# Attention steps that run on across head groups, and query units with three 256-wide products in half a PSUM bank a tile

## What is computed

```python
# layer 0: sliding-window attention with sinks; layer 1: NSA attention; after each a conv FFN
proj = h @ w_in                      # h: 256 x 2048; 32 query heads of 64, in 4 groups of 8
s = q @ k.T - slope * dist           # per head, 256 queries x up to 256 keys
p = softmax(s)                       # layer 0: with a sink in the denominator
o = p @ v                            # layer 1: gate0*o_cmp + gate1*o_sel + gate2*o_win
mix = o @ w_o
x = x + rmsnorm(mix, g[1])
h = rmsnorm(x, g[2])
x = x + rmsnorm((silu(conv(h @ w_gate)) * (h @ w_up)) @ w_down, g[3])
```

## Time and profile before

| what | value |
|---|---|
| median of 3 runs | 2227.19 us (2223.99 to 2230.46) |
| the profiled execution's own time | 2230.99 us |
| its span, first to last instruction | 2229.3 us |
| PE matmul busy | 2167.5 us (97%) |
| DVE, ACT, POOL busy | 1353.7, 1084.3, 249.9 us |
| mean granted TensorE clock | 0.987 |
| DMA | 381.14 MB, mean 171 GB/s |

### The profile page before, as it was taken

How to read it: one execution, slowest core, us unless ns; L and a number is a source line. 1 busy time by engine, 2 the same in 40 slices (tenths; PEclk the granted TensorE clock), 3 DMA queues, 4 the chain that set the end, 5 groups by cost and what they waited for, 6 DMA issues and landing times.

```text
span 2229.3 us, 34314 instructions
## 1 busy us (share of the span) xinstructions
PE 2167.5 (97%) x11619; PEld 1807.2 (81%) x11619; DVE 1353.7 (61%) x2087; ACT 1084.3 (49%) x1639; POOL 249.9 (11%) x395
## 2 busy tenths in 40 slices
PE   8999999999999999999989998999999999999998
PEld 7777888888888888888777776888888888888887
DVE  7655577676767654447754444467666766664444
ACT  6765454444444444445455555454444444443443
POOL 3351000000000000003005544000000000000000
PEclk9999999999999999999999999999999999999999
DMA  6434545656565565554562222545555555565553
GB/s 210 138 122 170 189 152 179 198 179 197 173 201 181 192 207 189 189 189 167 174 208 76 69 73 86 179 160 184 186 189 186 188 188 182 194 207 189 189 188 124
DMA packets 107195, 381.14 MB, mean 171 GB/s; under 512 B 14114, under 2 KB 14578, under 8 KB 106482
## 3 DMA queue, kind: packets, MB, share of 16 engines
q1 hardware_dynamic: 104962, 373.69, 50.5%
q10 hardware_dynamic: 2160, 6.46, 0.8%
HBM read 377.97 MB, written 2.14 MB: 171 GB/s over the span
## 4 chain that ended last, share of the span: by engine, by line
PE 91%; DVE 5%; issue 2%; ACT 1%; POOL 1%; DMA 0%; DVEq 0%; ACTq 0%; POOLq 0%; SPq 0%
PE set L541 36%; PE set L609 29%; PE set L545 18%; PE set L727 2%; PE set L709 1%; PE set L750 1%; DVE wlo L1302 1%; DVE scored L1579 1%; PE set L638 1%; POOL probs L496 1%; PE set L711 1%; PE set L743 0%; PE set L702 0%; PE set L753 0%; ACT whi L935 0%
## 5 line engine op out<-in xcount | busy, mean ns | idle before, releaser
L541 PE MATMUL set<-hs,whi 128*128 128x512 f32 x3584 | 1215.5, 402 | 18.6 <-DVE wlo L1302 7.1
L1302 DVE TENSOR_TENSOR wlo<-raw,whi 128x1024 fp32r<-128x1024 f32 x704 | 857.9, 1229 | 564.8 <-ACT whi L935 563.6
L935 ACT ACTIVATE whi<-raw 128x1024 fp32r<-128x1024 f32 x704 | 738.9, 1057 | 764.5 <-PE set L545 408.8
L545 PE MATMUL set<-hs,wlo 128*128 128x256 f32 x3584 | 853.9, 281 | 0.0
L545 PEld LDWEIGHTS set<-hs,wlo 128*128 128x128 f32 x3584 | 672.9, 190 | 78.1
L541 PEld LDWEIGHTS set<-hs,whi 128*128 128x128 f32 x3584 | 620.7, 190 | 115.3 <-issue 15.6
L609 PE MATMUL set<-whi,hid 128*128 128x512 f32 x1408 | 387.0, 395 | 0.0
L609 PEld LDWEIGHTS set<-whi,hid 128*128 128x128 f32 x1408 | 264.6, 188 | 63.5 <-DVE wlo L1302 0.6
L609 PE MATMUL set<-wlo,hid 128*128 128x512 f32 x704 | 222.4, 395 | 0.0
L609 PEld LDWEIGHTS set<-wlo,hid 128*128 128x128 f32 x704 | 132.4, 188 | 31.6
L609 PE MATMUL set<-whi,os 128*128 128x512 f32 x512 | 145.7, 398 | 0.0
(11 more groups left out here) (180 smaller groups left out, 1194.9 us busy)
## 6 DMA issues: line engine op xcount, KB each, us to landing
raw<-in_stream SPq DMA_DIRECT2D x704, 512.0 KB, 3.3
gain_rows<-rows ACTq DMA_DIRECT2D x4, 1024.0 KB, 5.2
xT<-in_x SPq DMA_DIRECT2D x8, 256.0 KB, 8.2
out_y<-out_f SPq DMA_DIRECT2D x3, 512.0 KB, 2.7
bo_rows<-rows ACTq DMA_DIRECT2D x1, 1024.0 KB, 8.0
wg_raw<-in_w_gates ACTq DMA_DIRECT2D x1, 768.0 KB, 4.3
out_y<-out_f SPq DMA_DIRECT2D x2, 256.0 KB, 2.4
w2k_sb<-in_w ACTq DMA_DIRECT2D x2, 128.0 KB, 7.6
```

Of the source, the lines that this page charges most:

```text
L541: return mm(sets[set_of(u)][:, t, 0:2 * w], whi[:, slot, cols], r, start=first, stop=final)
L545: return mm(sets[set_of(u)][:, t, w:2 * w], wlo[:, slot, cols], r[:, 0:w], start=False, stop=False)
L935: A(whi[:, slot, :], raw[:, slot, :], ACT.Copy).then_inc(hi_ready, 1)
L1302: V.tensor_tensor(wlo[:, slot, :], raw[:, slot, :], whi[:, slot, :].bitcast(F32), ALU.subtract).then_inc(lo_ready, 1)
```

## The change

1. The loops over g are written out, so operands are addressed directly (`k_dup`, `v_nat`, `kc_all`, `gates`, `sinks_sb`), and `stage` and its tiles are gone. POOL keeps only the product that makes `vc_g` (`mask_values`).
2. `attention_steps` numbers the pairs of a layer through: step m of the next group follows on the last one of the group before, at an even distance of 32 slots per group (layer 0: 4 slots a half step; layer 1: 1.78), starting at slot 3. The fill is in the first group and the drain after the last one only. In the output unit the last group's half steps stand in slots 3 to 23.
3. `q_unit` replaces `unit` for the queries: three matmuls of 256 columns per tile and k-tile (`whi` x high, `whi` x low, `wlo` x high), all summed in the same half bank. Four tiles take two banks, and successive query units alternate between banks 0, 1 and banks 2, 3; each waits only for the unit before the last.
4. ACT has no part in reading the queries out. DVE makes `qg` from PSUM in one pass: layer 0 four `tensor_scalar` of 256 columns, layer 1 two `scalar_tensor_tensor` of 512 columns. The first two tiles end half a k-tile earlier (`q_first`).

```diff
-def attention_slots(layer, last):
-    halves = 2 * (len(attention_pairs(layer)) + LAG + 1)
-    lo, hi = (0, 23) if last else (1, 30)
-    at = [[] for _ in range(CH * UT)]
-    for k in range(halves):
-        at[lo + k * (hi - lo) // (halves - 1)].append((k // 2, k % 2))
-    return at
+def attention_steps(layer):
+    per, slots = len(attention_pairs(layer)), CH * UT
+    last = (GROUPS - 1) * per
+    final = 2 * (per + LAG + 1) - 1
+    at = [[[] for _ in range(slots)] for _ in range(GROUPS)]
+    for k in range(2 * (GROUPS * per + LAG + 1)):
+        m, h = divmod(k, 2)
+        if m < last:
+            slot = FIRST_SLOT + k * slots // (2 * per)
+        else:
+            slot = (GROUPS - 1) * slots + FIRST_SLOT + (k - 2 * last) * (LAST_SLOT - FIRST_SLOT) // final
+        at[slot // slots][slot % slots].append((m, h))
+    return at
...
+            def q_unit(u, waits=None, tile_before=None, after_chunk=None):
+                g = (u - Q0) if u < O0 else (u - Q1)
+                banks = [2 * (g % 2), 2 * (g % 2) + 1]
+                for c in range(CH):
...
+                    for j in range(CK):
+                        kt = CK * c + j
+                        r = hs[:, kt, :]
+                        if kt == KT - 1:
+                            turns = [(t, i) for t in range(UT) for i in range(3)]
+                        else:
+                            turns = [(t + a, i) for t in (0, 1) for i in range(3) for a in (0, 2)]
+                        for n, (t, i) in enumerate(turns):
+                            if tile_before and n % 6 == 0:
+                                tile_before(c * UT + j * CK + n // 6)
+                            if kt == 0 and n == 0:
+                                if g >= 2:
+                                    pe.wait_ge(evacuated, UT * (u - 1))
...
+                            w = (wlo if i == 2 else whi)[:, slot, cols]
+                            ins = mm(sets[0][:, banks[t // 2], (t % 2) * S:(t % 2 + 1) * S], w, r[:, S:2 * S] if i == 1 else r[:, 0:S],
+                                     start=kt == 0 and i == 0 and t % 2 == 0, stop=kt == KT - 1 and i == 2 and t % 2 == 1)
...
-                with pe.Fori(0, GROUPS - 1) as g:
-                    unit(q0 + 1, hs, lp=(g, CH, UT), tile_before=attention(layer, g * UT + UT * (q0 + 1), g, False))
+                for g in range(GROUPS - 1):
+                    q_unit(q0 + 1 + g, tile_before=attention(layer, g))
...
-                    add(0)
-                    for t in range(UT):
-                        if t + 1 < UT:
-                            add(t + 1)
-                        dve.wait_ge(q_summed, more_e + (UT * (u - q0) + t + 1))
-                        V.scalar_tensor_tensor(qg[:, t, :], half[:, st, t, :], -HD ** -0.5, rnorm[:],
-                                               ALU.mult, ALU.mult).then_inc(evacuated, 1)
+                        bank = sets[0][:, 2 * (g % 2) + half_unit, :]
+                        if layer == 1:
+                            V.scalar_tensor_tensor(qg[:, 2 * half_unit:2 * half_unit + 2, :],
+                                                   bank.rearrange("p (t s) -> p t s", t=2), -HD ** -0.5, row_of_r(2),
+                                                   ALU.mult, ALU.mult).then_inc(evacuated, 2)
+                            continue
```

More of the change, by code:

```diff
@@ L84, in halves_before @@
 def halves_before(u):
-    return UT * (u - sum(u >= b for base in (O0, DN0, O1, DN1) for b in range(base + 1, base + 5)))
+    without = [b for base in (O0, DN0, O1, DN1) for b in range(base, base + 4)]
+    without += [b for base in (Q0, Q1) for b in range(base, base + GROUPS)]
+    return UT * sum(v not in without for v in range(u))
 def attention_items(layer):
@@ L509, in next_bias @@
                         nc.gpsimd.tensor_scalar(t, t, 0.25, 1.0, ALU.mult, ALU.mult).then_inc(bias_ready, 1)
[L511 to L517 removed]
+                for m in range(PAIRS[layer]):
+                    normalize(m)
+                    next_bias(m)
+                    if pair_item(layer, m)[1] == "cmp" and m > 0:
+                        mask_values(group_pair(layer, m)[0])
                 ff = FF0 if layer == 0 else FF1
@@ new lines, in attention, with scores @@
+            def attention(layer, host):
+                items = attention_items(layer)
+                q0 = (Q0, Q1)[layer]
+                at = attention_steps(layer)[host]
+                def scores(m):
+                    i, kind = pair_item(layer, m)
+                    g = group_pair(layer, m)[0]
+                    if m >= 1:
+                        pe.wait_ge(scores_read, item(layer, m, 0))
+                    if m == 0:
+                        pe.wait_ge(k_dup_ready, 1 if layer == 0 else 3)
@@ L1137, in step @@
+                def step(tile):
+                    for m, h in at[tile]:
+                        o = m - LAG - 1
+                        if h == 1 and o >= 0 and pair_item(layer, o)[1] in ("swa", "win"):
                             pair_high(o)
-                        if LAG <= n < len(pairs) + LAG and h < len(pairs[n - LAG]):
-                            copy_turned(n - LAG, h)
-                        if n < len(pairs) and h < len(pairs[n]):
-                            exponents(n, h)
@@ L1143, in attention, with attention_unit @@
-                return step
-            def attention_unit(u, evac, step, lp=None):
-                more, turn, _ = loop_terms(lp)
+                        if LAG <= m < PAIRS[layer] + LAG and h < len(pair_heads(layer, m - LAG)):
+                            copy_turned(m - LAG, h)
+                        if m < PAIRS[layer] and h < len(pair_heads(layer, m)):
+                            exponents(m, h)
+                return step
+            def attention_unit(u, evac, step):
                 g0 = first_chunk(u)
@@ L1246, in _ @@
                     act.dma_start(rows.rearrange("n (k f) -> (n k) f", f=P), post_rows[0:5 * KT, :]).then_inc(rows_made, 16)
-                with act.Fori(0, GROUPS - 1) as g:
-                    lp = (g, CH, UT)
-                    attention_unit(q0 + 1, q_evac(q0 + 1, lp), attention(layer, g, False), lp)
+                for g in range(GROUPS - 1):
+                    attention_unit(q0 + 1 + g, lambda: None, attention(layer, g))
                 n = 2 * layer
```

407 lines of the change are left out of this document (187 added, 220 removed).

## The result

| | before | after |
|---|---|---|
| median | 2228.82 us (2223.99 to 2231.96, 4 runs) | 2190.69 us (2188.55 to 2193.26, 4 runs) |
| span of the profiled execution | 2229.3 us | 2191.5 us |
| ratio | | 0.9837, 95% interval 0.9815 to 0.986 |

The kernel is 38.1 us faster by the medians (36 by the ratio, whose interval is about 31 to 41). The two profiled executions differ by 37.8 us of span. The prediction said 2196, in a range of 2181 to 2214.

A forecast was written before the change was run, and what follows sets the result against it. PE, busy 97% of the span, was taken as the bound. Savings of 11.5, 8.7 and 12.2 us less losses of 1.0 and 0.5 gave -30.9 us, 2200 profiled, 2196 after taking off 3.8; range 2181 to 2214.

The forecast's parts named there:

- The likeliest case: Whole kernel: the terms as summed, 2196 us, own range 2188 to 2204, chance 0.58.
- a: Query-unit starts: alternating banks remove PE's waits for DVE to clear PSUM, 12.2 us less 0.7 left; 11.5 us saved.
- b: Query hosts: steps that run on cut PE's 11.7 us of waits for probabilities to 3.0; 8.7 us saved.
- c: Layer 1, 1172 to 1345: clock falls (mean 0.92) after the removed waits go, except one; 12.2 us saved.
- d: Layer 1's output unit: missing fill saves, closer steps and doubled turns cost; 1.0 us lost, bounds 6 saved, 8 lost.
- e: Query units: three 256-column products with three loads replace 512 plus 256 with two; 0.5 us lost in all.
- Every sign named for them: No unit-start wait for `qg`, at most tenths in slot 3; layer 1 query-host POOL waits under 3 us, longest group 0.
- The rival that the chain binds again: Attention flow: DVE, ACT and POOL need the 3.6 us left, b saves nothing, half of c returns; 2210 us, chance 0.20.
- The fall that was left for group 0: Layer 1's pipeline fill: one clock fall stays after a 1.5 us wait, priced at 1.6 us.
- the 5 to 9 foretold: Layer 1's output unit: 5 to 9 us of PE waits would remain, most of them for POOL.
- 3 x 0.117 = 0.351: Query units: three 256-column products at 0.117 us each take 0.351 us, against 0.350 for the former pair.
- slow rival: Query units: weight loads not hidden between 256-column products; at 0.190 us each, 112 us more, 2308 us; chance 0.08.

The follow-up runs named there:

- wide product run: Changed kernel with a tile's two 256-column high-weight products in the query units made one of 512 (query values differ): 2187.07 us, ratio 0.9824.

## Why the prediction was right, and where its terms were off

The likeliest case came, with 5 us more than it said. Term by term, measured between the two profiled executions, which are 37.8 us apart:

| term | predicted | measured | from |
|---|---|---|---|
| a, b: PE's idle time | -20.2 | -19.8 | windows: 7.5 in layer 0, 11.1 in layer 1's hosts; 1.2 at the joint ahead of them |
| c: clock | -12.2 | -12.4 | 161.4 less 149.0 |
| d: output unit | +1.0 | 0.0 | idle +0.6 in layer 1, -0.5 in layer 0 |
| e: 256-wide products | +0.5 | +3.6 to +4.7 | wide product run |
| left out | 0 | about -10 | the remainder |

**a and b.** Every sign named for them came: no wait for `qg` at a unit's start or in slot 3, waits for POOL in the query hosts of layer 1 of 2.8 us, the longest (1.30) in group 0. The sum of a and b was right, their split was not. (Of the 4.1 us that b read for layer 0's query hosts, 1.4 stand in its output unit.) The prediction subtracted each wait from its own row, as if one could be had without the other. With the banks alone idle time in layer 1's hosts falls by 1.5 us (slots 3 to 30) or 3.8 us (slots 1 to 30) and the turns' waits grow; with the steps alone it falls by 8.6; with both by 11.1. The rival that the chain binds again, 2210 us, is close to what happens with the banks alone (2213 and 2211). It didn't come in the changed kernel; b's account, that steps that run on just give the chain the time that it needs (3.6 us against 3.6), fits the waits that are left, which are small but not gone.

**c.** The size was right for the profiled execution, and the fills show that it is the clock and not something that goes with the waits: the same products behind the same joints, with PE kept busy, took 8.0 us less. The fall that was left for group 0 (a wait of 1.5 us in the fill) didn't come, and the wait was 1.3. What c told too simply is which waits bring a fall. With one pair of banks a wait of 1.9 us was left and the clock stayed at 1.00, of three waits of 2.0 us with the banks alone one had a fall behind it, and nearly the same waits brought a mean clock of 0.92 in one execution and 0.95 in another. The term was worked out from one execution in which it was larger than in the other; had that one been profiled, it would have been 8. The sum then took this execution's 3.8 us over the median off once more. But executions of the kernel before are slow when their clock is low (0.987 in the profiled one, 0.990 in the median of the others), so most of the 3.8 is likely the same falls, which c had already removed. The terms by themselves end nearer to 2200 than to 2196. That 2196 is only 5 us off is in part luck: taken off twice, the 3.8 us stood in for some of the gain that was left out.

**d.** The waits of the output unit are 6.4 us (4.4 + 1.6 + 0.4), inside the 5 to 9 foretold and mostly for POOL, and the 1.6 at the first doubled turn is twice the 0.8 taken; at the second it is 0.83, listed under POOL. The gain from the missing fill made up for it. The density of the steps was a cost, as d said, and a slot number takes half of it back.

**e.** The step that failed is "3 x 0.117 = 0.351". The distance is 0.119 to 0.120. It comes with the third product and its load: the order of the products changes nothing, and two products with two loads take it away. Which of the two it is stays open. Nothing like the slow rival's prices (0.190) showed. The Trainium skill (TensorE: Matmul & The Clock Gate, "The mechanism") has a load overlap a matmul under way only if its row group differs, and by it the prediction estimated 55 us for the added loads. Here a load and a product more in each tile and k-tile cost 0.007 to 0.009 us with the row group the same, so in these runs the measurement decides against this rule. The same section of the Trainium skill also lets PE pull a load ahead when it goes to the background weight buffer, which the prediction passed over; the measurement fits that, but no run here shows the buffer.

**What was left out.** Of the remainder, 37.8 less about 28, two parts can be sized. Waits count for more than the table says: in the changed kernel's timeline the turn at 1177.02 is listed with 1.30 us, and the product ahead of it started at 1175.44, 1.58 us before, where 0.12 is usual; so 1.46 us were lost, of which 0.16 lie beneath the recorded end of that product. The attention's waits were 30 and are 15, so 2.4 us. Scores and outputs that stand in one step save 0.18 us by the run that parts them. Before, one step in each group of layer 0 held both, four in all; after, 13 do. That is 9 more, 1.6 us. In layer 1 the number grows by 9 as well, but the run that parts them found nothing in its hosts, so nothing is put down for them. The prediction had named this gain and left it out of the sum. The Trainium skill (TensorEngine Tiling (Array Packing), "Key Properties") says that a change of tiling mode drains the engine; the trace agrees so far that in the changed kernel the three products of the turn at 81.60 are 0.11 apart and the scores, 64 rows deep, start at 82.02, 0.20 us after the last of them. These two parts are some 4 us. About 6 us have no place; the interval of the ratio is 5 us either way, so this is not shown to be anything.

## What to carry to other kernels

Two waits in a row on one engine are not two gains: take one away and the engine reaches the next sooner, so price a pair of edits together, and take the gain of each alone from a run. What a slow clock costs is busy time at 1.00 against busy time at the mean seen, and it belongs to the execution that was profiled; look at a second one before it goes into a sum, and don't also take off what the profiled one was slower than the median. When a fill or a drain is spread out, look for two half steps that fall into one slot: here one slot number was worth 3 us.

## What the runs showed of the hardware

- The clock's falls differ between executions with the same waits (mean 0.92 and 0.95 in layer 1's hosts). A wait of 1.9 us by itself didn't bring one, and of three waits of 2.0 us in one run one had a fall to 0.50 behind it. Over executions of the kernel before, the time went with the mean clock: 2221.5 us at 0.994, up to 2234.3 at 0.987. Keeping TensorE busy with idle products in waits of 1.6 to 1.9 us ended the falls there and gained 4.9 us by the medians, but fills longer than the wait gave it all back.
- An f32 product of 128 x 128 by 128 columns is recorded as two passes and takes 0.22 us (16 passes in 1.76 us), twice what the count in the code suggests.
- Products of 256 columns with a load each follow at 0.119 us where three stand in place of one of 512 and one of 256, and the region that they add to has no part in it.
